# A decoder step on one core: four projection units beside each weight chunk instead of two, and the step's input and weights loaded in turns

## The reference, cut to what matters

```python
def trunk_layer(x, pos0, pool_prefix, attend, norm1_g, w_in, ...):
    h = rms_norm(x, norm1_g)
    u, q, k, v, iq, ik, iw = project(h, pos, w_in, q_norm_g, k_norm_g)   # z = h @ w_in, 1024 -> 1864
    ya, pool_state = pool_mix(u, pool_prefix, pos0, w_pool, pool_scale)
    yb = attend(q, k, v, iq, ik, iw)
    x = x + jnp.concatenate([ya, yb], axis=-1) @ w_o
    x = x + peer(rms_norm(x, norm2_g), w_pq, sub_keys, expert_u, expert_v)
    return x, k, v, ik, pool_state

def project(h, pos, w_in, q_norm_g, k_norm_g):
    z = h @ w_in
    ...
    q = rope(rms_norm(q, q_norm_g), pos); k = rope(rms_norm(k, k_norm_g), pos)
    iq = rope(iq, pos); ik = rope(ik, pos)

def dsa_block(q, iq, iw, qpos, idx_keys, k_sel, gather_kv):
    s = jnp.einsum('bqhd,bld->bqhl', iq, idx_keys)            # indexer: 8 heads x 64
    score = jnp.einsum('bqhl,bqh->bql', relu(s), iw)
    top_val, top_idx = lax.top_k(where(admissible, score, -inf), k_sel)
    ...                                                        # softmax attention over the chosen keys
```

## Time and profile before

| | |
|---|---|
| median of 3 executions | 978.09 us |
| lowest, highest | 977.93, 984.63 us |
| the profiled execution, its time | 981.52 us |
| its span, first to last instruction | 980.0 us |
| TensorE busy | 959.5 us, 98% |
| VectorE / ScalarE / GpSimd busy | 764.0 / 558.2 / 437.0 us |
| mean granted clock | 0.998 |

### The profile page before, as it was taken

The page is one execution under the profiler, slowest core; times in us unless marked ns, Lnnn a source line. Parts: engine busy times, 40 slices in busy tenths (PEclk is TensorE's granted clock), DMA queues, the critical chain, the costliest instruction groups (busy, mean ns, idle before and its releaser), DMA issues.

```text
span 980.0 us, 18911 instructions
## 1 busy us (share of the span) xinstructions
PE 959.5 (98%) x6440; PEld 836.3 (85%) x6440; DVE 764.0 (78%) x1785; ACT 558.2 (57%) x1092; POOL 437.0 (45%) x328
## 2 busy tenths in 40 slices
PE   5999999999999999999999999999999999999998
PEld 2346879999899999999999998888888888888887
DVE  2469965369999938999999976687888878888873
ACT  2122445454355559999999975654555555555552
POOL 3644365245778886777677770021212211212100
PEclk9999999999999999999999999999999999999999
DMA  9625658668765554444444557898888888888873
GB/s 330 148 90 173 215 170 301 216 230 309 273 175 187 174 181 161 153 153 162 160 151 159 164 164 224 257 333 291 296 298 306 302 272 301 301 307 300 303 255 96
DMA packets 75442, 221.53 MB, mean 226 GB/s; under 512 B 11301, under 2 KB 23725, under 8 KB 74964
## 3 DMA queue, kind: packets, MB, share of 16 engines
q1 hardware_dynamic: 60812, 179.12, 54.3%
q0 software_dynamic: 12800, 40.36, 13.2%
q10 hardware_dynamic: 1744, 0.92, 0.4%
HBM read 217.41 MB, written 3.14 MB: 225 GB/s over the span
## 4 chain that ended last, share of the span: by engine, by line
PE 91%; DVE 3%; DMA 2%; ACTq 2%; issue 1%; ACT 1%; SPq 0%
PE psum L1120 36%; PE psum L1059 22%; PE psum L1060 12%; PE psum L1071 3%; PE psum L1055 3%; PE psum L872 2%; PE psum L603 2%; PE psum L788 1%; PE psum L820 1%; ACTq L402 1%; PE psum L873 1%; DMA w_slice<-w_pq_cols 1%; PE psum L581 1%; DMA w_rest<-w_in_blocks 1%; PE psum L887 1%
## 5 line engine op out<-in xcount | busy, mean ns | idle before, releaser
L1627 POOL TENSOR_TENSOR w_lo<-w_raw,w_hi 128x1024 fp32r<-128x1024 f32 x116 | 279.2, 2413 | 123.3 <-ACT w_hi L1167 123.3
L1059 PE MATMUL psum<-h_split,w_hi 128*128 128x256 f32 x1792 | 327.0, 284 | 2.3 <-issue 2.3
L1060 PE MATMUL psum<-h_split,w_lo 128*128 128x256 f32 x1024 | 289.4, 283 | 0.0
L1059 PEld LDWEIGHTS psum<-h_split,w_hi 128*128 128x128 f32 x1792 | 279.2, 192 | 3.8 <-issue 3.6
L1167 ACT ACTIVATE w_hi<-w_raw 128x1024 fp32r<-128x1024 f32 x214 | 224.9, 1051 | 41.9 <-DMA w_raw<-expert_ut 32.5
L1060 PEld LDWEIGHTS psum<-h_split,w_lo 128*128 128x128 f32 x1024 | 196.1, 192 | 0.0
L2150 DVE TENSOR_TENSOR w_lo<-w_raw,w_hi 128x1024 fp32r<-128x1024 f32 x98 | 120.4, 1229 | 58.3 <-ACT w_hi L1167 58.1
L1120 PE MATMUL psum<-w_hi,ag_hi 128*128 128x512 f32 x512 | 158.1, 389 | 0.0
L1120 PE MATMUL psum<-w_hi,ag_lo 128*128 128x512 f32 x512 | 157.9, 389 | 0.0
L1167 ACT ACTIVATE ag_hi<-store 128x256 fp32r<-128x256 f32 x128 | 53.2, 417 | 157.3 <-PE psum L1120 157.3
L1120 PEld LDWEIGHTS psum<-w_hi,ag_lo 128*128 128x128 f32 x512 | 96.1, 188 | 19.9
(11 more groups left out here) (349 smaller groups left out, 1475.9 us busy)
## 6 DMA issues: line engine op xcount, KB each, us to landing
w_raw<-expert_ut SPq DMA_DIRECT2D x128, 512.0 KB
w_raw<-expert_v SPq DMA_DIRECT2D x86, 512.0 KB
raw_more<-expert_v SPq DMA_DIRECT2D x42, 512.0 KB, 4.9
w_slice<-w_pq_cols SPq DMA_DIRECT2D x32, 512.0 KB, 4.8
w_most<-w_in_blocks SPq DMA_DIRECT2D x8, 699.0 KB, 10.6
w_slice<-w_o_half SPq DMA_DIRECT2D x8, 512.0 KB, 4.9
v_cache<-cache_v POOLq DMA_DIRECT2D x64, 64.0 KB, 3.7
w_o_sb<-w_o_half SPq DMA_DIRECT2D x8, 512.0 KB, 6.1
```

The source lines that it names most:

```text
L1059: pe.matmul(out, w_hi[:, s, c, :], h_split[:, c, a], start=(c == 0 and a == 0), stop=False)
L1060: mm = pe.matmul(out, w_lo[:, s, c, :], h_split[:, c, 0], start=False, stop=(c == KC - 1), skip_group_check=wide)
L1627: pool.tensor_tensor(w_lo[:, s], w_raw[:, s], w_hi[:, s].bitcast(F32), ALU.subtract).then_inc(S["w_lo_ready"], 1)
```

## The change

1. SP issues each of the four loads of `xT` just ahead of a weight chunk, instead of all four first.
2. The page table and the gains are loaded by ScalarE's queue, not GpSimd's. ScalarE no longer squares `xT` (VectorE does, 128x576 a time), and issues its 20 indexer pages before it takes the root for the token norm, once weight chunk 1 is in.
3. GpSimd issues the small tables after weight chunk 2 is in and ahead of its indexer pages, and two of them (`gain5`, the prompt's `rope`) after these. Its rotation of prompt tile 0 waits for VectorE's `rope_qk(0)`, and its `diag0` waits for `rope_qk(2)`.
4. The loop over arriving chunks does four prompt units (0 to 3) and the sample unit; `token_ssq` moves from chunk 0 to chunk 5 and into another bank. The four left over are cut into smaller pieces: twelve matmuls ahead of the transposes of the samples' heads, four after them, and so on.
5. VectorE does `rope_qk(2)` ahead of the samples' sort, not after eleven of its steps. ScalarE's copies are put in the order that this asks for.

```diff
@@ sync
-            for k in range(0, KC, 2):
-                sp.dma_start(xT[:, k:k + 2, :], x_t[:, k:k + 2, :]).then_inc(S[f"x_in{k // 2}"], 16)
             for k in range(KC):
+                if k < KC // 2:
+                    sp.dma_start(xT[:, 2 * k:2 * k + 2, :], x_t[:, 2 * k:2 * k + 2, :]).then_inc(S[f"x_in{k}"], 16)
                 sp.dma_start(w_most[:, k], w_in_blocks[k, :, 0:3, :]).then_inc(S[f"w_in_in{k}"], 16)
@@ tensor
-                for i in range(2):
+                for i in range(4):
                     mm = z_unit(i, k)
...
-                if k == 0:
+                if k == 5:
                     token_ssq()
...
-            z_prompt(2)
             pe.wait_ge(S["rstd_half"], 1)
-            z_prompt(3)
+            z_prompt(4)
+            z_prompt(5, 0, KC // 2)
...
-            z_prompt(4, 0, KC // 2)
+            z_prompt(5, KC // 2)
...
                 if g == 0:
-                    z_prompt(4, KC // 2)
-            z_prompt(5, 0, 2)
+                    z_prompt(6, 0, KC // 2)
+            z_prompt(6, KC // 2, 6)
...
-            z_prompt(5, 2)
+            z_prompt(6, 6)
...
             prompt_heads(0)
-            z_prompt(6)
+            z_prompt(7, 0, 2)
...
             prompt_idx(0)
-            z_prompt(7, 0, 2)
+            z_prompt(7, 2, 4)
             prompt_heads(1)
-            z_prompt(7, 2, KC // 2)
+            z_prompt(7, 4, 6)
             prompt_sums(0)
             prompt_idx(1)
-            z_prompt(7, KC // 2)
+            z_prompt(7, 6)
@@ scalar
-            for c in range(KC):
-                act.wait_ge(S[f"x_in{c // 2}"], 16)
-                act.activation(sq[:, c, :], xT[:, c, :], ACT.Square).then_inc(S["sq_ready"], 1)
+            for dst, src in gain_loads:
+                act.dma_start(dst, src).then_inc(S["gains_in"], 16)
+            act.wait_ge(S["gains_in"], 16 * len(gain_loads))
+            act.wait_ge(S["w_in_in1"], 32)
+            ik_loads(act, W_IK[0] + W_IK[1], W_IK[2])
+
             act.wait_ge(S["rstd_half"], 1)
             act.activation(rstd_a[:, 0:12], rstd_b[:, 0:12], ACT.Sqrt).then_inc(S["rstd_root"], 1)
-
-            act.wait_ge(S["gains_in"], 16 * len(gain_loads))
-            ik_loads(act, W_IK[0] + W_IK[1], W_IK[2])
@@ gpsimd
+                if i == 1:
+                    pool.wait_ge(S["rope_done"], 1)
+                    pool.wait_ge(S["consts_in"], 16 * len(early_loads + next_loads))
...
+            pool.wait_ge(S["rope_done"], 3)
             pool.wait_ge(S["zp_done"], 6)
@@ vector
                 if c % 2 == 1:
-                    dve.wait_ge(S["sq_ready"], c + 1)
+                    settle(dve.tensor_tensor(sq[:, c - 1:c + 1, :], xT[:, c - 1:c + 1, :], xT[:, c - 1:c + 1, :], ALU.mult))
...
+            rope_qk(2)
             dve.wait_ge(S["score_s_copied"], 1)
...
-            sort(11)
-            rope_qk(2)
-            sort(10)
+            sort(21)
             select_p(0)
```

More of the change, by code:

```diff
@@ L383, in hybrid_kernel @@
     early_loads = [
-        (rope[0:NS, 2, :], c_rope[SEQ:NT, :]), (rope[:, 0:2, :], c_rope[0:SEQ, :].rearrange("(t p) c -> p t c", p=P)),
-        (fold[:], c_fold), (causal_new[:], c_causal_new), (own[:], c_own), (iota[:], c_iota),
-        (gain5[:], head_gains),
+        (rope[0:NS, 2, :], c_rope[SEQ:NT, :]), (fold[:], c_fold), (causal_new[:], c_causal_new), (own[:], c_own),
+        (iota[:], c_iota),
+    ]
+    next_loads = [
+        (gain5[:], head_gains), (rope[:, 0:2, :], c_rope[0:SEQ, :].rearrange("(t p) c -> p t c", p=P)),
     ]
@@ L588, in token_ssq @@
                 for t in range(2):
-                    pe.matmul(psum[:, 4, 4 * t:4 * t + 4], sq[:, 0, t * P:(t + 1) * P], ones[:, 0:4], start=True,
+                    pe.matmul(psum[:, 1, 4 * t:4 * t + 4], sq[:, 0, t * P:(t + 1) * P], ones[:, 0:4], start=True,
                               stop=True, skip_group_check=True)
                 for j in range(4):
-                    mm = pe.matmul(psum[32 * j:32 * j + 32, 4, 8:12], sq[:, 0, SEQ:NT], ones[:, 0:4], start=True,
+                    mm = pe.matmul(psum[32 * j:32 * j + 32, 1, 8:12], sq[:, 0, SEQ:NT], ones[:, 0:4], start=True,
                                    stop=True, tile_position=(0, 32 * j), skip_group_check=True)
@@ L1210, in _ @@
             copy_z(1)
-            head_root(0, NS)
             copy_z(2)
             copy_z(3)
+            head_root(0, NS)
+            copy_z(4)
             act.wait_ge(S["heads_s_psum"], 1)
@@ L1225, in _ @@
             head_root(1, P)
+            copy_z(5)
             relu_s(0)
-            copy_z(4)
             relu_s(1)
+            head_root(2, P)
             act.wait_ge(S["score_s_psum"], 1)
             copy(score4[:, :], psum[:, 0, 0:QW]).then_inc(S["score_s_copied"], 1)
-            copy_z(5)
             copy_heads(0)
-            head_root(2, P)
             copy_z(6)
@@ L1540, in _ @@
             pool.memset(ones[:, :], 1.0).then_inc(S["ones_set"], 1)
-            for dst, src in gain_loads:
-                pool.dma_start(dst, src).then_inc(S["gains_in"], 16)
+            pool.wait_ge(S["w_in_in2"], 32)
+            for dst, src in early_loads:
+                pool.dma_start(dst, src).then_inc(S["consts_in"], 16)
             pool.wait_ge(S["gains_in"], 16 * len(gain_loads))
             ik_loads(pool, W_IK[0], W_IK[1], "ik_in_pool")
-            for dst, src in early_loads:
+            pool.wait_ge(S["consts_in"], 16 * len(early_loads))
+            for dst, src in next_loads:
                 pool.dma_start(dst, src).then_inc(S["consts_in"], 16)
-            pool.wait_ge(S["consts_in"], 16 * len(early_loads))
             for i, t in enumerate(ORDER):
@@ L1695, in _ @@
             dve.wait_ge(S["ssq_done"], 1)
-            inverse_mean(rstd_b[:, 0:12], psum[:, 4, 0:12], D, S["rstd_half"])
+            inverse_mean(rstd_b[:, 0:12], psum[:, 1, 0:12], D, S["rstd_half"])
             def rope_qk(i):
@@ L1711, in rope_qk @@
                 settle(dve.tensor_tensor(x, x, bc(small[0:n, 16:16 + NH + 1], 2, HD), ALU.mult))
-                dve.wait_ge(S["consts_in"], 16 * len(early_loads))
+                dve.wait_ge(S["consts_in"], 16 * len(early_loads + next_loads))
                 settle(dve.tensor_tensor(x, x, gain5[0:n], ALU.mult))
```

## The result

| | before | after |
|---|---|---|
| median, us | 978.75 (20 runs, 977.01 to 984.63) | 984.84 (20 runs, 978.25 to 987.71) |
| ratio, 95% interval | | 1.0045 (1.003 to 1.0059) |
| the profiled execution, its time | 981.52 us | 984.18 us |
| its span and mean clock | 980.0 us, 0.998 | 982.7 us, 0.991 |

The change costs about half a per cent. The 20 times of after fall into two groups by the mean clock of the run: seven at 0.996 to 0.997 took 978.25 to 981.33 us (median 979.88), thirteen at 0.991 took 984.18 to 987.71 (median 985.60). The profiled run is the fastest of the second group. The median lies in the second group, so it moved by 6.1 us; the mean moved by 4.6.

A forecast was written before the change was run, and what follows sets the result against it. TensorE bounds the kernel, with gains only in its first 125 us. The 3.1 us earlier start and removed waits are absorbed by SP's queue and VectorE's mask, leaving +0.4: 978.09 + 0.4 = 978.5 us, range 975.0 to 981.3.

The forecast's parts named there:

- The start: First weight chunk: TensorE starts at 7.5 us instead of 10.58, a gain of 3.1 us.
- Three ends meet: Forecast (a), up to slice 4: SP's queue and VectorE's mask eat the earlier start; +0.4, 978.5 us, chance 0.55.
- the first chunk: Loop over arriving chunks: first chunk takes 4.27 us plus some 2.8 us for half clock, as before.
- Where TensorE ends up: At the first logits: TensorE arrives at 87.2 us, waits 6.7 for the mask at 93.9; overall +0.4 us taken.
- rival d: Behind the mask: clock falls as in the first chunk, 2.8 us instead of 1.9; +1.8, 979.9 us, chance 0.07.
- the stretch after 49.84: Behind the samples' transposes before the change: 0.66 clock cost 1.9 us, expected to go; also used to price the mask wait.
- The rule that I cited: Behind the mask wait: half rate is default, idle TensorE falls back to it until sustained work; +0.9 or +1.5.
- nothing moves by over 1%: Whole kernel: within 1% (9.8 us) of no change, chance 0.95; faster 0.02, slower 0.03.
- third rival: Prediction gave it +1.5; third listed, (c), is a wait at the samples' transposes passed on by SP: 980.1, chance 0.13.

The follow-up runs named there:

- the late mask: Kernel before, ten more sorting steps ahead of the first mask; its profile repeats the unchanged part up to the first logits. 985.55 us, ratio 1.0075.
- the clock held up: Changed kernel with six dummy 466-column matmuls in TensorE's wait for the first mask: 978.43 us, ratio 1.0001.
- mask and band products first: Changed kernel, masks after 13 sorting steps, band products ahead of first logits, slices 1 to 3 after 16 pages: 979.85 us; with slice 4 also earlier, 978.17 us.
- dense work behind the same wait: Changed kernel with four dummy 466-column matmuls between the first logits and the band products: 982.39 us, ratio 1.0039.
- the root ahead: Kernel before with the change's loads, token-norm root after 8 of ScalarE's 20 pages: 981.4 us; with three sorting steps moved behind the last rotation too, 981.35 us.
- the mask first: Changed kernel with VectorE's first mask after 13 sorting steps instead of 21, the second right behind it: 980.92 us, ratio 1.0026.
- half the filling: Changed kernel with three dummy 466-column matmuls instead of six in the wait ahead of the first logits: 982.24 us, ratio 1.0031.
- the last experiment: Kernel before with the change's loads, token-norm root after 16 of ScalarE's 20 pages, shorter sort ahead of the last rotation: 975.42 us, ratio 0.9973.

## Why the prediction was wrong

Right by its steps:

- **The start.** 6.51 us against 7.5; no idle time at the transposes and no fall of the clock behind them. (The kernel before doesn't have these two in every execution either: see the late mask.)
- **Three ends meet.** TensorE was at the first logits at 86.27 us (forecast 87.2) and waited 5.25 us (forecast 6.7) for VectorE. With the clock held up, the time is that of before (978.43 us). That it also meets the 978.5 is partly luck, since the mask came 2.5 us sooner than forecast and the base was wrong (below).

Off in size, without harm: the scores ended at 63.53 instead of 65.5 us (1.0 us of it the start, 0.9 the first chunk: 12.69 - 6.51 = 6.18 us instead of 4.27 + 2.8), and from there to slice 4 SP took 51.35 us instead of 52.8, so it issued the slice at 114.88 instead of 118.35. With the 4.1 us to landing it had 7 us to spare, and so was not one of the ends in this profile. But 6.8 of the 7 are the slow stretch itself: without it SP would have been in time by some 0.4 us, and with mask and band products first TensorE did wait 3.00 us for this slice. The mask came at 91.41 instead of 93.9, 1.7 us of it since VectorE's copy ended earlier (42.56 against 44.3), 1.3 since the third rotation took 7.0 us (63.05 to 70.0) and not 8.3; the other steps took 0.5 more.

**The step that failed** is in "Where TensorE ends up": "if the stretch behind it runs as after 49.84, 1.9 us, the 11.3 us become 13.2". The mechanism was right and the term mis-sized: the stretch took 18.09 us, 6.8 more and not 1.9 (or the 2.8 of rival d). Both of my rows for a fall, the first chunk and the stretch after 49.84, have 466-column matmuls behind them. The first is not even a fall by the granted clock: its matmuls are slow by their records (0.96 us against 0.56), but the profile has the clock at 1.00 there. Behind the mask stand logits and band products, and there the clock stayed down over these and over the 288-column matmuls of 102.18 to 106.16 us. That the small matmuls have a part in the long fall is shown by what happened with dense ones in their place: none in 34 runs (10 with dense work behind the same wait, 24 with the root ahead, where the wait is at another place), against 13 of 20 in the changed kernel, 6 of 12 with the mask first, 6 of 10 with half the filling, and 3 of 5 with the late mask. Why it comes in some runs and not in others, and what it is in the small matmuls that allows it, isn't shown. The rule that I cited from the Trainium skill, "TensorE: Matmul & The Clock Gate", Part 1, was right on the fall in this profile (behind the wait of 2.93 us with half the filling the profile has none). As to its end, the same part has sustained work lift the clock; here it was still down after 14 us of work without a gap in the records, and the measurement decides.

A second step: the shift was worked out against the profiled execution and then put on the median. The profiled execution of before pays for the slow stretch at 50 to 55 us, but most runs of before have a higher mean clock than its 0.998 (14 of the 20 beside the last experiment), so the 1.9 us that I let the change take away there were not in the median. By the second view of before (in the late mask) the 1.07 us at the transposes and 1.4 us of the start need not have been there either. All of the 3.43 us by which the profiled execution is above the median stand inside its span: the 1.5 us outside are in every run. Profile to profile the change costs 2.7 us, median to median 6.1.

With both put right, and the measured mask: after the change TensorE is at the second logits at 91.5 + 18.1 = 109.6 us. In a run of before without the slow stretch it is there at 106.20 - 1.9 = 104.3 us, or, from the second view, at 90.97 + 11.28 = 102.3. That is 5.3 or 7.4 us later, with 6.1 measured between the medians. The clock decides whether the forecast fails: the seven runs with the higher clock have a median of 979.88 us, inside the range of 975.0 to 981.3, the thirteen others are all above it.

That nothing moves by over 1% was right, and so was the rival in which the clock behind the mask makes it slower (d); its chance of 0.07 and its price of 1.8 us were both too small. (The "+1.5 of the third rival" in the prediction is the price of no rival; (d) has 1.8.)

## What to carry to other kernels

- An idle time on TensorE that "only" absorbs time won elsewhere is not always free. Price the fall of the clock by the work that stands behind the wait: here some 2 us ahead of 466-column matmuls, and 1.7 (mask first) to 6.8 us ahead of small ones. If a wait can't be avoided, put it ahead of dense work, or move independent work into it.
- Before a shift is put on a median, ask which of the profiled execution's waits and slow stretches the median run has. Two profiles of the same instructions differed by 4 us after 62 us here.
- A step that is moved on an in-order queue is priced by everything that now stands ahead of something else: a root moved 7 us forward lost 5.5 us for another root. With that root after 16 pages instead of 8, the loads of the change and the shorter sort, the kernel was 0.3% faster than before.

## What the runs showed of the hardware that I had not expected

- The granted clock stayed at 0.50 for some 17 us (89.1 to 106.1), about 14.6 of them with TensorE at work, at one wait of 5.25 us; at a wait of 2.80 us, ahead of the same matmuls, it was back after 3.4 us.
- Short or long is open from run to run. That makes two groups of times out of one kernel, their medians 5.7 us apart: 978.25 to 981.33 and 984.18 to 987.71 us after the change.
- Whether there is a fall isn't settled by the length of the wait alone: in the profiles there is none behind 1.60 and 2.93 us (half of the filling), one behind 1.07 us, 2.80, 3.00, 3.74, 3.98 and 5.25 us.
- In the first chunk the 466-column matmuls took 0.96 us against 0.56 later, with a granted clock of 1.00 in the profile of the stretch (10 to 17 us before, 6 to 13 us after). What slows them the profile doesn't say.
